# adaLN blocks one place ahead in a diffusion trunk, and a pool residual without ScalarE's bias step

## What is computed

```python
mod = (silu(cond) @ w_ada[i] + b_ada[i])[:, None, :]
sh1, sc1, g1, sh2, sc2, g2 = jnp.split(mod, 6, axis=-1)
h = rmsnorm(x, norm_g[i, 0]) * (1.0 + sc1) + sh1
y = mixer_i(h)             # Hyena, gated linear attention, FNet, pool
x = x + g1 * y
h = rmsnorm(x, norm_g[i, 1]) * (1.0 + sc2) + sh2
x = x + g2 * hier_moe(h)   # 16 experts, top 2 of the best group of 4
```

## Time and profile before

| | |
|---|---|
| median of 3 runs | 1438.69 us |
| profiled execution | 1437.99 us |
| its span | 1436.2 us |
| mean granted clock of TensorE | 0.991 |
| moved from HBM | 549 MB, 384 GB/s over the span |

### The profile page before, as it was taken

How to read it: one execution, slowest core, us unless ns; L and a number is a source line. 1 busy time by engine, 2 the same in 40 slices (tenths; PEclk the granted TensorE clock), 3 DMA queues, 4 the chain that set the end, 5 groups by cost and what they waited for, 6 DMA issues and landing times.

```text
span 1436.2 us, 17316 instructions
## 1 busy us (share of the span) xinstructions
PE 1357.9 (95%) x7234; PEld 734.6 (51%) x7234; DVE 361.1 (25%) x883; ACT 286.8 (20%) x523; POOL 36.4 (3%) x36
## 2 busy tenths in 40 slices
PE   7999999999989999999999989999998887999986
PEld 3786584444325788774444336744443353444433
DVE  3444514112113313323111113331111144111113
ACT  3211024111102221232111004421110054111101
POOL 0001310000000000010000000100000000000000
PEclk9999999999999999999999999999999997999998
DMA  9956999999999983499999999999999999999994
GB/s 377 420 194 226 404 398 384 395 424 429 427 427 421 421 371 103 186 410 385 396 427 427 428 426 420 421 428 421 426 428 428 426 419 401 383 427 428 427 428 167
DMA packets 54213, 552.28 MB, mean 385 GB/s; under 512 B 5937, under 2 KB 7921, under 8 KB 8817
## 3 DMA queue, kind: packets, MB, share of 16 engines
q1 hardware_dynamic: 52496, 549.09, 91.8%
q10 hardware_dynamic: 1634, 2.02, 0.4%
HBM read 548.99 MB, written 2.10 MB: 384 GB/s over the span
## 4 chain that ended last, share of the span: by engine, by line
PE 80%; DMA 15%; DVE 2%; ACT 1%; issue 0%; POOL 0%; SPq 0%; POOLq 0%; DVEq 0%
PE bank L720 25%; PE bank L666 14%; DMA ring<-in_moe_w 12%; PE bank L744 12%; PE bank L626 5%; PE bank L685 4%; PE bank L703 3%; DMA ring<-in_pool_w 2%; PE bank L497 2%; PE bank L514 2%; PE bank L640 1%; PE bank L840 1%; PE bank L952 1%; PE bank L572 1%; PE bank L727 1%; PE bank L890 1%
## 5 line engine op out<-in xcount | busy, mean ns | idle before, releaser
L720 PE MATMUL bank<-ring,arena 128*64 128x512 f32 x1024 | 229.4, 595 | 33.0 <-DMA ring<-in_moe_w 31.4
L720 PE MATMUL bank<-ring,hT 128*64 128x512 f32 x1024 | 225.3, 594 | 0.0
L744 PE MATMUL bank<-ring,arena 128*64 128x512 f32 x896 | 198.8, 596 | 0.0
L720 PEld LDWEIGHTS bank<-ring,arena 128*64 128x64 f32 x1024 | 73.1, 137 | 181.6 <-issue 151.4
L720 PEld LDWEIGHTS bank<-ring,hT 128*64 128x64 f32 x1024 | 72.1, 137 | 139.3 <-issue 137.0
L1430 DVE TENSOR_TENSOR rows<-rows,bank 128x512 f32<-128x512 f32 x32 | 22.0, 688 | 469.4 <-PE bank L720 469.4
L744 PEld LDWEIGHTS bank<-ring,arena 128*64 128x64 f32 x896 | 61.2, 137 | 117.6 <-issue 112.0
L666 PE MATMUL bank<-hT,ring 128*128 128x256 f32 x512 | 112.4, 380 | 0.0
L666 PEld LDWEIGHTS bank<-hT,ring 128*128 128x128 f32 x512 | 96.5, 190 | 15.2 <-issue 2.5
L1152 ACT ACTIVATE yv_big<-bank,arena 128x512 fp32r<-128x512 f32 x64 | 44.0, 688 | 288.6 <-PE bank L744 288.6
L1449 DVE SCALAR_TENSOR_TENSOR yv_rest<-bank,arena,yv_big 128x512 fp32r<-128x512 f32 x64 | 48.1, 751 | 200.1 <-ACT yv_big L1152 200.1
(11 more groups left out here) (215 smaller groups left out, 1225.7 us busy)
## 6 DMA issues: line engine op xcount, KB each, us to landing
ring<-in_moe_w SPq DMA_DIRECT2D x166, 2048.0 KB, 19.4
ring<-in_w_ada SPq DMA_DIRECT2D x96, 1024.0 KB, 22.5
ring<-in_moe_w SPq DMA_DIRECT2D x36, 1024.0 KB, 20.3
arena<-in_moe_w SPq DMA_DIRECT2D x16, 1024.0 KB, 19.6
ring<-in_hy_w_in SPq DMA_DIRECT2D x12, 1024.0 KB, 28.0
ring<-in_hy_w_out SPq DMA_DIRECT2D x4, 1024.0 KB, 12.0
ring<-in_gla_w_v SPq DMA_DIRECT2D x4, 1024.0 KB, 22.7
ring<-in_gla_w_g SPq DMA_DIRECT2D x4, 1024.0 KB, 16.5
```

The costliest lines, as they stand in the source:

```text
L720: last = mm(bank[4 + kind][SLOTS * e:SLOTS * e + SLOTS, :], x[:, k, at:at + SLOTS], w[:, kk, e, :], start=k == 0, stop=k == KD - 1)
L744: last = mm(bank[6 + q // 2][SLOTS * e:SLOTS * e + SLOTS, :], hidT[:, f, SLOTS * e:SLOTS * e + SLOTS], w[:, ff, e, :], start=f == 0, stop= ...
```

## The change

Blocks are renumbered places, not renumbered contents. Block 1 moves from the transforms of the first mixer to its input projection, one piece ahead of every second tile from tile 8 on; blocks 2, 3, 4 take the places of 1, 2, 3, and 5 that of 4. In the gated mixer, 6 and 7 take the places of 5 and 6, block 8 gets a new place between v and the second gate product, 9 that of 7, 10 that of 8. FNet's 9 becomes 11, and the places of 10 (beside layer 2's norm and router) and 11 (pool mixer) are empty. The stream has the same order of pieces. The pool residual loses ScalarE's step: VectorE first adds scale * g1 * b to all of x in one instruction, then adds each window tile times scale * g1 straight from PSUM; the second norm of layer 3 is summed by TensorE over eight tiles, without GpSimd.

```diff
+POOLED = (1, 3, 5)
...
-    before = [ada(0) + pieces("w_in", 12) + ada(1) + ada(2) + ada(3) + pieces("w_out", 4) + ada(4),
-              ada(5, 0, 5) + pieces("wq", 2) + ada(5, 5) + pieces("wk", 2) + ada(6) + pieces("wv", 4)
-              + pieces("wg", 4) + ada(7) + pieces("wo", 4) + ada(8),
-              ada(9) + pieces("fn", 4) + ada(10),
-              ada(11, 0, 5) + pieces("pool", 1) + ada(11, 5)]
+    w_in = pieces("w_in", 12)
+    between = [what for k in range(KD) for what in ada(1, k, k + 1) + w_in[4 + k:5 + k]]
+    before = [ada(0) + w_in[0:4] + between + ada(2) + ada(3) + ada(4) + pieces("w_out", 4) + ada(5),
+              ada(6, 0, 5) + pieces("wq", 2) + ada(6, 5) + pieces("wk", 2) + ada(7) + pieces("wv", 4)
+              + ada(8) + pieces("wg", 4) + ada(9) + pieces("wo", 4) + ada(10),
+              ada(11) + pieces("fn", 4),
+              pieces("pool", 1)]
...
             for c in range(4):
+                if c == 2:
+                    ada_turned(7)
...
-            ada_turned(6)
+            ada(8, 0, 8)
             gates(pe, 1)
+            ada_turned(8)
             pe.wait_ge(s("v_ready"), 4)
...
-                pe.wait_ge(s("mod_ready"), 7)
+                pe.wait_ge(s("mod_ready"), 9)
...
-                if n % 2:
+                if n in POOLED:
                     pe.wait_ge(s("squares_added"), (KD - 2) * (n // 2 + 1))
-                for k in (0, KD - 1) if n % 2 else range(KD):
+                for k in (0, KD - 1) if n in POOLED else range(KD):
...
             for m in range(24):
+                if m >= 8 and m % 2 == 0:
+                    ada(1, m // 2 - 4, m // 2 - 3)
...
             to_rows(0)
-            ada(1, 0, 1)
+            ada(2, 0, 1)
+            ada_turned(1)
             forward(0)
...
-            residual(2, "fn", rhs=fnm, beside=10)
-            moe(2, 10)
-
-
-            ada(11, 0, 2)
+            residual(2, "fn", rhs=fnm)
+            moe(2)
+
+
             norm(6)
-            ada(11, 2, 5)
...
-            ada(11, 5, 8)
             pe.wait_ge(s("mix_rows"), 12 + 4)
...
-                if m == 1:
-                    ada_turned(11)
...
-            residual(3, "pool_b", half)
+            load_log_exp()
+            act_fn(minus[:], ident, ACT.Copy, scale=-1.0)
+            for m in range(KD):
+                square(7, m)
...
+            ada_rows(1)
+            ada_mod(1)
             dve.wait_ge(s("conv_ready"), 24)
...
+            chain(tt(gs, mod[:, 3, 16:24], wide("pool_scale"), ALU.mult))
+            chain(tt(gb, gs, wide("pool_b"), ALU.mult))
+            chain(tt(xT[:], xT[:], gb.unsqueeze(3).broadcast_to([P, KD, G, L]), ALU.add))
+            for m in range(KD):
+                dve.wait_ge(s("res_mm"), KD * 3 + (m | 1) + 1)
+                for g in range(G):
+                    last = stt(xT[:, m, g], half(m)[:, g * L:g * L + L], gs[:, m, g:g + 1], xT[:, m, g],
+                               ALU.mult, ALU.add)
+                last.then_inc(s("x_added"), 1)
...
-            add_squares(7)
```

More of the change, by code:

```diff
@@ L311, in build @@
         g_bank = lambda m: 6 if m in (3, 5) else 7
-        ada_bank = lambda n: bank[6 if n == 2 else 7]
+        ada_bank = lambda n: bank[6 if n in (1, 3) else 7]
         block = ctx.enter_context(nc.Block())
@@ L480, in pe_gla @@
         def pe_gla(pe, arrived, ada, ada_turned, norm, h_ready, project, residual):
-            ada(5, 0, 2)
+            ada(6, 0, 2)
             norm(2)
-            ada(5, 2, 5)
+            ada(6, 2, 5)
             pe.wait_ge(s("cm_loaded"), 16)
@@ L501, in pe_gla @@
                 if w == 0:
-                    ada(5, 5, 8)
+                    ada(6, 5, 8)
                     gates(pe, 0)
-                    ada_turned(5)
-            ada(6, 0, 8)
+                    ada_turned(6)
+            ada(7, 0, 8)
             for c in range(4):
+                if c == 2:
+                    ada_turned(7)
                 w8 = arrived(("wv", c), KD)
@@ L584, in pe_gla @@
             pe.wait_ge(s("g_raw"), 8)
-            ada(7, 0, 3)
+            ada(9, 0, 3)
             pe.wait_ge(s("upd_read"), 6)
@@ L594, in pe_gla @@
                     last.then_inc(s("osum_mm"), 1)
-            ada(7, 3, 8)
-            residual(1, "wo", oT, lambda k: pe.wait_ge(s("o_ready"), k + 1), turned=7, beside=8)
+            ada(9, 3, 8)
+            residual(1, "wo", oT, lambda k: pe.wait_ge(s("o_ready"), k + 1), turned=9, beside=10)
         def gates(pe, d):
@@ L621, in ada @@
                 if lo == 0 and n:
-                    pe.wait_ge(s("mod_ready"), {2: 1, 3: 2}.get(n, n))
+                    pe.wait_ge(s("mod_ready"), {2: 1, 3: 2, 4: 3}.get(n, n))
                 for k in range(lo, hi):
@@ L967, in _ @@
             to_rows(0)
-            ada(1, 0, 1)
+            ada(2, 0, 1)
+            ada_turned(1)
             forward(0)
             to_rows(1)
-            ada(1, 1, 5)
+            ada(2, 1, 5)
             forward(1)
             inverse(0)
-            ada(1, 5, 8)
-            ada(2, 0, 3)
+            ada(2, 5, 8)
+            ada(3, 0, 3)
             to_rows(2)
-            ada_turned(1)
-            ada(2, 3, 4)
+            ada_turned(2)
+            ada(3, 3, 4)
             forward(2)
             inverse(1)
-            ada(2, 4, 8)
-            ada(3, 0, 2)
+            ada(3, 4, 8)
+            ada(4, 0, 2)
             to_rows(3)
-            ada_turned(2)
-            ada(3, 2, 3)
+            ada_turned(3)
+            ada(4, 2, 3)
             forward(3)
             inverse(2)
-            ada(3, 3, 8)
+            ada(4, 3, 8)
             inverse(3)
-            ada_turned(3)
+            ada_turned(4)
             pe.wait_ge(s("z_ready"), 4)
-            residual(0, "w_out", rhs=uT, beside=4)
-            moe(0, 4)
+            residual(0, "w_out", rhs=uT, beside=5)
+            moe(0, 5)
             pe_gla(pe, arrived, ada, ada_turned, norm, h_ready, project, residual)
-            moe(1, 8)
-            ada(9, 0, 2)
+            moe(1, 10)
+            ada(11, 0, 2)
             norm(4)
-            ada(9, 2, 5)
+            ada(11, 2, 5)
             pe.wait_ge(s("cm_loaded"), 16 * 2)
@@ L1016, in _ @@
                     last.then_inc(s("mix_mm"), 1)
-            ada(9, 5, 8)
+            ada(11, 5, 8)
             pe.wait_ge(s("mix_rows"), 8)
@@ L1742, in states @@
                 last.then_inc(s("upd_read"), 1)
-            ada_rows(5)
-            ada_mod(5)
+            ada_rows(6)
+            ada_mod(6)
             cumulate(0)
@@ L1749, in _ @@
             v.memset(sc[:], 0.0).then_inc(s("sc_clear"), 1)
-            ada_rows(6)
-            ada_mod(6)
+            ada_rows(7)
+            ada_mod(7)
+            ada_rows(8)
+            ada_mod(8)
             scores(0)
```

37 lines of the change are left out of this document (17 added, 20 removed).

## The result

The changed kernel takes **1443.38 us** (median of 7 runs, 1441.78 to 1444.03) against 1438.45 for the kernel before on the same chip (1436.82 to 1440.27, 7 runs). The ratio is 1.0034, with a 95% interval of 1.0024 to 1.0044: slower by 4.9 us, 0.34%. That is inside the predicted range of 1435.8 to 1444.2, and 3.4 us above the predicted 1440.0; it belongs to "slower by over 0.2%", which had a chance of 0.30. The profiled execution took 1442.9 us with a span of 1440.7, against 1437.99 and 1436.2.

The account below looks back on a forecast made before the run. TensorE (busy 95%) and the weight stream were both taken as nearly saturated, with full-ring MoEs gaining nothing from fewer bytes. Terms summed to +1.3 us, giving 1440.0 us from the 1438.69 median, range 1435.8 to 1444.2.

Parts of the forecast that it names:

- a piece alone costs 0.99 us: First mixer's projection: eight single adaLN pieces at 0.99 us each add +7.9 us, bounds 7.0 and 8.5.
- Gated mixer, +7.9: Gated mixer: one block more costs +7.0, one more turn +0.4, a wait for the new modulation +0.5.
- Layer 2's start, +0.5: From the g tiles to layer 2's MoE: -1.0 for the block removed, +1.5 for the low clock.
- The norm's gain (-0.6): Layer 2's second norm: one piece fewer ahead of the last sum of squares, -0.6 us, between 0 and -1.0.
- the covered router: Layer 2's router: VectorE's chain covers most of the block taken out, so nothing is gained there.
- The price of the low clock: Layer 2's first gathers: without adaLN pieces in the router they run at lower clock, +1.5 us, as in layer 3.
- Layer 2's MoE, -2.5: Layer 2's MoE: 8 MiB fewer ahead, so its ring starts full, -2.5 us, bounds 0 and -3.3.
- what would show it: List of signs, among them projection 92 us, layer 2's MoE near 210, transfers idle before layer 3's MoE.
- The first rival: Both late MoEs: freed transfers count in full, -15.7 instead of -2.5 us, giving 1426.8; chance 0.08.
- Layer 3's start, -13.0: Layer 3 before its MoE: pieces gone and new pool residual, -12.7 us; router products, -0.3.
- the second rival: Layer 3's pool stretch and layer 2's second norm: low clock spreads, 3.6 us more, giving 1443.6; chance 0.30.
- The -0.3 for the router products: Layer 3's router: its products no longer start at the low clock, -0.3 us.

Follow-up runs that it names:

- four pairs: Changed kernel with block 1's pieces in four pairs, ahead of every fourth projection tile, instead of eight single ones: 1440.44 us.
- one run: Changed kernel with block 1 as eight pieces in a row after tile 15 of the projection, instead of eight single ones: 1439.45 us.
- The run with zeros: Changed kernel with 18 products of zeros, whose results are never read, added in each router of layers 2 and 3: 1439.03 us.

## Why the prediction was right or wrong

**Right in the mechanism, 3.4 us too low in the sum.** The answer from the profile was that TensorE's own work sets the end in both mixers, that the late blocks were hidden or half hidden where they stood, and that the freed transfers are worth little. All three hold.

*The term "a piece alone costs 0.99 us" was too small.* In the projection it costs 1.19: +9.5 instead of +7.9, above the upper bound of 8.5. The piece's own time was right (1.00 from start to start); that the tiles around it would keep their pace was not. The two rows that gave 0.99 (922.69 and 923.68 in the earlier trace rows) can't show this: they end with the piece, and there is a wait ahead of it that could take in the change from another kind of product. Eight pieces, four pairs and one run gave 93.5, 92.2 and 91.2 us: 0.3 for each interruption, on top of the work.

*Gated mixer, +7.9:* measured +7.9.

*Layer 2's start, +0.5 forecast, +1.6 measured.* The norm's gain (-0.6) and the covered router (nothing gained: 11.85) came as said. The price of the low clock was mis-sized. The step took 1.5 us from layer 3; layer 2's gathers took 6.62 against 4.06 for the gathers of layer 1 in the same trace, 2.6 more, since here the clock stayed at 0.50 through most of them (956 to 962). In pairs and one run it was 1.5 and 1.4, so the 1.5 of the forecast came from one execution of a quantity that varies. The run with zeros showed the cause: 2.2 us back.

*Layer 2's MoE, -2.5:* measured -2.5, with a queue that stood still before it (8 GB/s over 958 to 960). Ahead of layer 3's MoE, too, the transfers went idle, as the part on what would show it had said. The first rival, freed transfers in full, fell: TensorE's waiting for weights went from 31.4 to 29.6 us, and layer 3's MoE kept its 208.2. The ring with two slots fewer showed what does set that length.

*Layer 3's start, -13.0 forecast, -11.6 measured.* First norm, residual, x + b and sums came as worked out, and GpSimd is out of the chain. The pool product ended 1.1 us later than the step had it, 0.8 of it by a clock of 0.57, the rest by h. That is the second rival, in one of the places it named and at a fifth of its 3.6 us there; with the 1.0 more than forecast in layer 2's gathers it came to about half of it. The -0.3 for the router products did not come (4.40 us again in the earlier trace rows and after): they stand behind a wait of 2.16 as before.

*The class.* Forecast +1.3 with 0.53 on no change; measured +4.9. Of the 3.6 us between them 1.6 is the price of interruptions, and 1.0 and 0.8 the low clock in layers 2 and 3; what is left are small terms of both signs. The measured time lay inside the range without errors that cancel: all three point the same way. But the chance of 0.30 for slower hung on the clock almost alone (0.27 of it), and nearly half of the miss came from a term that I had bounded too tightly.

## What to carry to other kernels

Work that is moved earlier must land under a wait; a block under VectorE's router chain was free, the same block in a stretch where TensorE has no gap costs its full length, and 0.3 us more each time it interrupts a run of other products. Ask of every transfer that is taken away whether the buffer ahead of the stage was already full: if it was, the bytes were free, and only time on the engine before the stage counts. And work taken out of a wait has one more price, the engine's clock after it: here 36 products of zeros, 18 in each of two routers, took 3 to 4 us off. They help only what stands behind them, and how long the clock stays low varies, so a price read from one execution is good to a microsecond at best.

## What I had not expected of the hardware

- A change between two kinds of product on TensorE and back costs some 0.3 us though neither waits for data: 8.10 us for two tiles and a piece, of which 6.96 (27.84 / 4) and 0.88 (7.00 / 8, inside a run of eight) are the parts' own; and a projection of 91.2, 92.2 and 93.5 us with one, four and eight interruptions.
- The lower clock strikes the same place in one kernel and not in the next: the pool product took 8.83 us with a granted clock of 0.57 and 8.06 with 1.00, with the same instructions and the same 2.20 us of waiting ahead.
- The clock fell where TensorE never waited long: in layer 2 of the changed kernel its longest waits from the norm to the gathers were 1.23, 2.23, 1.93 and 1.18 us, and the granted clock was 0.50 over 945 to 948 and over 956 to 962.
- One VectorE instruction over 2048 elements a partition took 2.29 us, 1.12 ns an element, where four of the 512 elements that I bounded it by would be 2.8.
